# Forget gate kept as eight rows: a narrow projection, one scan over time, and its bias in the attention logits as a 128-row matmul

## The reference, cut to what matters

```python
def hybrid_mixer(h, w_in, b_f, ...):
    z = h @ w_in                                  # 256 x 4616
    zp, zq, zk, zv, zf, zx, zy = jnp.split(z, offsets, axis=-1)
    y_attn = forgetting_attention(zq, zk, zv, zf, b_f)   # zf: 256 x 8
# forgetting_attention, per head, with t the query and s the key:
#   F = cumsum(log_sigmoid(zf + b_f), axis=time)
#   logits[t, s] = (q[t] . k[s]) * scale + F[t] - F[s]     for s <= t
#   softmax over s, times v
```

## Time and profile before

| | |
|---|---|
| median of 3 runs | 3135.54 us (3131.29 to 3140.22) |
| the profiled execution | 3136.8 us, of which the span in the trace is 3135.0 us |
| PE busy | 3096.4 us, 99% of the span |
| DVE busy | 1981.1 us, 63% |
| ACT busy | 1481.2 us, 47% |
| mean granted TensorE clock | 0.990 |

### The profile page before, as it was taken

How to read it: one execution, slowest core, us unless ns; L and a number is a source line. 1 busy time by engine, 2 the same in 40 slices (tenths; PEclk the granted TensorE clock), 3 DMA queues, 4 the chain that set the end, 5 groups by cost and what they waited for, 6 DMA issues and landing times.

```text
span 3135.0 us, 38941 instructions
## 1 busy us (share of the span) xinstructions
PE 3096.4 (99%) x14466; PEld 2576.0 (82%) x14466; DVE 1981.1 (63%) x2086; ACT 1481.2 (47%) x1740; POOL 106.6 (3%) x206
## 2 busy tenths in 40 slices
PE   8999989999999999999999999999999999999999
PEld 7887868888888888888888888888888888888887
DVE  6778778975655655865564565556475555565564
ACT  5244535544444444545444444544545454444543
POOL 1211110100000000000000000000000000000000
PEclk9989999999999999999999999999999999999999
DMA  9978887965555555455556545555554555545555
GB/s 373 371 300 306 295 305 255 359 224 189 187 188 188 180 194 186 166 181 168 192 173 194 190 147 192 178 184 187 170 181 166 195 173 190 174 162 194 167 186 190
DMA packets 179990, 658.46 MB, mean 210 GB/s; under 512 B 20080, under 2 KB 20368, under 8 KB 179216
## 3 DMA queue, kind: packets, MB, share of 16 engines
q1 hardware_dynamic: 150992, 550.51, 52.1%
q0 software_dynamic: 28864, 106.08, 9.0%
HBM read 654.41 MB, written 2.10 MB: 209 GB/s over the span
## 4 chain that ended last, share of the span: by engine, by line
PE 96%; DMA 2%; DVE 1%; ACT 1%; issue 0%; SPq 0%; DVEq 0%; ACTq 0%
PE pg L1037 29%; PE pg L1039 29%; PE pg L1038 29%; PE pm L1072 2%; DMA w_raw<-w 1%; PE pm L1100 1%; PE pm L1558 1%; DMA R<-w_ada 1%; PE pm L1127 1%; PE pm L1452 0%; PE pm L1178 0%; PE pm L1177 0%; PE pm L1240 0%; PE pm L1135 0%; ACT w_hi L592 0%
## 5 line engine op out<-in xcount | busy, mean ns | idle before, releaser
L1607 DVE TENSOR_TENSOR w_lo<-w_raw,w_hi 128x1024 fp32r<-128x1024 f32 x888 | 1085.8, 1225 | 973.1 <-ACT w_hi L510 967.9
L510 ACT ACTIVATE w_hi<-w_raw 128x1024 fp32r<-128x1024 f32 x888 | 940.8, 1060 | 1328.5 <-PE pg L1039 1295.5
L1037 PE MATMUL pg<-w_hi,hT_hi 128*128 128x512 f32 x3232 | 1280.9, 396 | 18.5 <-DVE w_lo L1765 8.1
L1039 PE MATMUL pg<-w_hi,hT_lo 128*128 128x512 f32 x3232 | 1264.9, 391 | 0.0
L1038 PE MATMUL pg<-w_lo,hT_hi 128*128 128x512 f32 x3232 | 1264.3, 391 | 0.0
L1037 PEld LDWEIGHTS pg<-w_hi,hT_hi 128*128 128x128 f32 x3232 | 611.6, 189 | 146.4 <-issue 10.4
L1039 PEld LDWEIGHTS pg<-w_hi,hT_lo 128*128 128x128 f32 x3232 | 610.4, 189 | 129.6
L1038 PEld LDWEIGHTS pg<-w_lo,hT_hi 128*128 128x128 f32 x3232 | 611.5, 189 | 123.4 <-issue 0.5
L1037 PE MATMUL pg<-w_hi,y_parts 128*128 128x512 f32 x864 | 337.9, 391 | 1.4 <-issue 1.4
L1039 PE MATMUL pg<-w_hi,y_parts 128*128 128x512 f32 x864 | 336.4, 389 | 0.0
L1038 PE MATMUL pg<-w_lo,y_parts 128*128 128x512 f32 x864 | 336.1, 389 | 0.0
(11 more groups left out here) (281 smaller groups left out, 1380.3 us busy)
## 6 DMA issues: line engine op xcount, KB each, us to landing
w_raw<-w SPq DMA_DIRECT2D x1028, 512.0 KB, 3.7
R<-w_ada POOLq DMA_DIRECT2D x196, 512.0 KB, 7.4
R<-mem_T SPq DMA_DIRECT2D x4, 512.0 KB, 7.2
x_rows<-x SPq DMA_DIRECT2D x1, 2048.0 KB, 16.2
R<-mem_T SPq DMA_DIRECT2D x1, 2048.0 KB, 11.3
out<-x_rows SPq DMA_DIRECT2D x4, 512.0 KB, 5.8
con_sb<-con SPq DMA_DIRECT2D x1, 1344.0 KB, 16.0
small_w_sb<-small_w POOLq DMA_DIRECT2D x2, 576.0 KB, 5.8
```

Of the source, the lines that this page charges most:

```text
L510: act.activation(w_hi[:, g % RING, :, :].rearrange("p c n -> p (c n)"), raw[:, g % RING, :], ACT.Copy).then_inc(hi_done, 1)
L1037: pe.matmul(out, hi, w_hi[:, slot, c, :], start=start, stop=False)
L1039: return pe.matmul(out, lo, w_hi[:, slot, c, :], start=False, stop=stop)
L1607: tt(flat(w_lo[:, g % RING, :, :]), raw[:, g % RING, :], flat(w_hi[:, g % RING, :, :]).bitcast(F32), ALU.subtract).then_inc(lo_done, 1)
```

## The change

The gate is computed with the 8 gates on partitions and time along the row. The loaded side of the projection is now the 8 gate columns, split into `wf_hi` (ACT, at 35) and `wf_lo` (DVE, at 36), and the moving side is the activations that are already split (`hT_hi`, `hT_lo`), 256 columns at a time. Bias, minimum, `Exp`, `Ln` and the last subtraction work on 8x256, and one scan on DVE sums over time and writes `-F` straight into `F_row`. Two small transposes on PE make `F_t`. `F_row` is set to zero over all 128 partitions early on (DVE, at 11), and the bias matmul of the logits reads all 128 of its rows. `tri` is gone, so `con1` halves from 512 to 256 KB.

```diff
-        zf, logf, F_t = (sc[:, 240 + 16 * i:256 + 16 * i].rearrange("p (a h) -> p a h", a=TB) for i in range(3))
-        b_f = sc[:, 288:296]
+        zf, logf = view(12, S)[0:8, :], view(13, S)[0:8, :]
+        wf_hi, wf_lo = view_r(5, KD, 8), view_r(5.5, KD, 8)
+        F_t = sc[:, 240:256].rearrange("p (a h) -> p a h", a=TB)
+        b_f = sc[0:8, 288:289]
...
+            upto(35)
+            act.wait_ge(fw_in, 32)
+            act.activation(flat(wf_hi), flat(w_f), ACT.Copy).then_inc(wf_hi_done, 1)
...
-            act.activation(F_row[0:8, :], pm[2][0:8, 0:S], ACT.Copy, scale=-1.0).then_inc(F_sb, 1)
-            act.activation(flat(F_t), pm[2][:, S:S + TB * 8], ACT.Copy).then_inc(F_sb, 1)
+            act.activation(flat(F_t), pm[2][:, 0:TB * 8], ACT.Copy, scale=-1.0).then_inc(F_sb, 1)
...
-                        i = pe.matmul(out, ident[0:8, forget + h:forget + h + 1].to_broadcast([8, P]), F_row[0:8, :],
+                        i = pe.matmul(out, ident[:, forget + h:forget + h + 1].to_broadcast([P, P]), F_row,
                                       start=False, stop=True)
...
-            for tb in range(TB):
-                for k in range(KD):
-                    i = pe.matmul(pm[2][:, tb * 8:(tb + 1) * 8], hf_1[:, k, tb * P:(tb + 1) * P], w_f[:, k, :],
-                                  start=(k == 0), stop=(k == KD - 1))
+            pe.wait_ge(wf_ready, 1)
+            for k in range(KD):
+                out = pm[2][0:8, 0:S]
+                pe.matmul(out, wf_hi[:, k, :], hT_hi[:, k, :], start=(k == 0), stop=False)
+                pe.matmul(out, wf_lo[:, k, :], hT_hi[:, k, :], start=False, stop=False)
+                i = pe.matmul(out, wf_hi[:, k, :], hT_lo[:, k, :], start=False, stop=(k == KD - 1))
...
-            for sb_ in range(TB):
-                pe.matmul(pm[2][0:8, 0:S], logf[:, sb_, :], tri[:, sb_, :], start=(sb_ == 0), stop=(sb_ == 1))
             for tb in range(TB):
-                for sb_ in range(tb + 1):
-                    i = pe.matmul(pm[2][:, S + tb * 8:S + (tb + 1) * 8], tri[:, sb_, tb * P:(tb + 1) * P],
-                                  logf[:, sb_, :], start=(sb_ == 0), stop=(sb_ == tb))
+                i = pe.transpose(pm[2][:, tb * 8:(tb + 1) * 8], F_row[0:8, tb * P:(tb + 1) * P], ident[0:8, 0:8])
...
+            step(dve.memset(F_row, 0.0))
...
+            upto(36)
+            dve.wait_ge(wf_hi_done, 1)
+            tt(flat(wf_lo), flat(w_f), flat(wf_hi).bitcast(F32), ALU.subtract).then_inc(wf_ready, 1)
...
-            step(tt(zf, pm[2][:, 0:TB * 8].rearrange("p (a h) -> p a h", a=TB),
-                    b_f.unsqueeze(1).to_broadcast([P, TB, 8]), ALU.add))
-            step.settle()
-            step(ts(flat(F_t), flat(zf), -1.0, None, ALU.mult))
+            step(ts(zf, pm[2][0:8, 0:S], b_f, None, ALU.add))
             step.settle()
-            tt(flat(logf), flat(zf), flat(F_t), ALU.min).then_inc(zf_in, 1)
+            stt(logf, zf, -1.0, zf, ALU.mult, ALU.min).then_inc(zf_in, 1)
             upto(41)
             dve.wait_ge(zf_out, 2)
-            stt(flat(logf), flat(zf), 0.0, flat(logf), ALU.min, ALU.subtract).then_inc(logf_ready, 1)
+            step(stt(logf, zf, 0.0, logf, ALU.min, ALU.subtract))
+            step.settle()
+            dve.tensor_tensor_scan(F_row[0:8, :], ones[0:8, 0:1].to_broadcast([8, S]), logf, 0.0, ALU.mult, ALU.subtract
+                                   ).then_inc(F_ready, 1)
```

More of the change, by code:

```diff
@@ L155 @@
 _at = 0
-for _name, _n in (("causal", TB * S), ("tri", TB * S)):
+for _name, _n in (("causal", TB * S),):
     CON1[_name] = (_at, _at + _n)
@@ L311, in build @@
         causal = con1[:, 0:TB * S].rearrange("p (a s) -> p a s", a=TB)
-        tri = con1[:, TB * S:2 * TB * S].rearrange("p (a s) -> p a s", a=TB)
         pool_w = mv[:, 1, 0, :].rearrange("p (g d) -> p g d", g=4)
         F_row = mv[:, 1, 1, 0:S]
-        zf, logf, F_t = (sc[:, 240 + 16 * i:256 + 16 * i].rearrange("p (a h) -> p a h", a=TB) for i in range(3))
-        b_f = sc[:, 288:296]
+        zf, logf = view(12, S)[0:8, :], view(13, S)[0:8, :]
+        wf_hi, wf_lo = view_r(5, KD, 8), view_r(5.5, KD, 8)
+        F_t = sc[:, 240:256].rearrange("p (a h) -> p a h", a=TB)
+        b_f = sc[0:8, 288:289]
         w_f = small_w[:, 0:KD * 8].rearrange("p (k n) -> p k n", n=8)
@@ L389, in build @@
         lam_in, lam_out = map(sem, ("lam_in", "lam_out"))
-        zf_ps, zf_in, zf_out, logf_ready, F_ps, F_sb = map(
-            sem, ("zf_ps", "zf_in", "zf_out", "logf_ready", "F_ps", "F_sb"))
+        zf_ps, zf_in, zf_out, F_ready, F_ps, F_sb, wf_hi_done, wf_ready = map(
+            sem, ("zf_ps", "zf_in", "zf_out", "F_ready", "F_ps", "F_sb", "wf_hi_done", "wf_ready"))
         pool_ps, pool_sb = map(sem, ("pool_ps", "pool_sb"))
@@ L449, in _ @@
                 if g == 26:
-                    sp.dma_start(b_f, t["b_f"].partition_broadcast(P)).then_inc(fw_in, 16)
+                    sp.dma_start(b_f, t["b_f"]).then_inc(fw_in, 16)
                     sp.dma_start(small_w[:, 0:KD * 8 + 8 * P], t["front_w"]).then_inc(fw_in, 16)
@@ L688, in _ @@
             act.wait_ge(zf_in, 1)
-            act.activation(flat(logf), flat(logf), ACT.Exp).then_inc(zf_out, 1)
+            act.activation(logf, logf, ACT.Exp).then_inc(zf_out, 1)
             act.wait_ge(zf_out, 1)
-            act.activation(flat(logf), flat(logf), ACT.Ln, bias=1.0).then_inc(zf_out, 1)
+            act.activation(logf, logf, ACT.Ln, bias=1.0).then_inc(zf_out, 1)
             upto(43)
@@ L1246, in _ @@
             upto(42)
-            pe.wait_ge(cons1_in, 16 * 2)
-            pe.wait_ge(logf_ready, 1)
-            for sb_ in range(TB):
-                pe.matmul(pm[2][0:8, 0:S], logf[:, sb_, :], tri[:, sb_, :], start=(sb_ == 0), stop=(sb_ == 1))
+            pe.wait_ge(F_ready, 1)
             for tb in range(TB):
-                for sb_ in range(tb + 1):
-                    i = pe.matmul(pm[2][:, S + tb * 8:S + (tb + 1) * 8], tri[:, sb_, tb * P:(tb + 1) * P],
-                                  logf[:, sb_, :], start=(sb_ == 0), stop=(sb_ == tb))
+                i = pe.transpose(pm[2][:, tb * 8:(tb + 1) * 8], F_row[0:8, tb * P:(tb + 1) * P], ident[0:8, 0:8])
             i.then_inc(F_ps, 1)
             upto(46)
-            pe.wait_ge(F_sb, 2)
+            pe.wait_ge(F_sb, 1)
             pe.wait_ge(evac_act, F_ACTS[FRONT.index("y")])
@@ L1921, in _ @@
             take_mod(5, 3)
-            dve.wait_ge(F_sb, 2)
+            dve.wait_ge(F_sb, 1)
+            dve.wait_ge(cons1_in, 16 * 2)
             attn_at(73, 0, S1, causal, 0)
@@ L2417, in constants @@
     con1[:, 0:TB * S] = np.where(s[None, None, :] <= t[:, :, None], 0.0, FAR).reshape(P, -1)
-    con1[:, TB * S:2 * TB * S] = (t[:, :, None] <= s[None, None, :]).reshape(P, -1)
     band = np.zeros((P, TB, 4, S), np.float32)
@@ L2504 @@
         "w_ada": np.stack(ada),
-        "b_f": a["b_f"][0], "final_g": a["final_g"],
+        "b_f": a["b_f"][0][:, None], "final_g": a["final_g"],
         "pool_w": a["pool_w"][0].transpose(1, 0, 2),
```

## The result

The changed kernel takes 3120.27 us (median of 5 runs, 3117.05 to 3122.06) against 3135.54 (5 runs, 3131.29 to 3140.22): ratio 0.9948, 95% interval 0.9933 to 0.9963. Its profiled execution took 3122.06 us, with a span of 3120.2 us: 14.8 less than the 3135.0 of before.

What follows compares the result with a forecast made beforehand. PE, busy for 99% of the span, was taken as the bound. 4.56 + 0.35 + 9.5 + 3.2 + 0.3 = 17.9 us off 3136.8 gives 3118.9, less 1.3 to the median, said as 3118; 3110 to 3126 holds 0.8.

Steps and rivals of the forecast that it cites:

- Projection: Gate projection on PE: 48 passes with 8 loaded columns take 5.83 us instead of 10.39, gaining 4.56 us.
- The rival of narrow passes that don't overlap: Gate projection: with 8 loaded columns each pass pays 0.2 us, 9.6 us more, 3127.5 us; chance 0.05.
- From the gate to tile 44: Projection's end to tile 44: shorter PE work would gain 2.7 us, but waiting for DVE leaves 0.35 us.
- the new wait: At tile 44: PE waits about 2.4 us for DVE's w_lo, as DVE has more to do ahead of it.
- elsewhere PE idled for 2.54 us in such a place and the clock stayed at 1.00: Wait at tile 44: one row elsewhere taken as sign that it costs 2.4 us alone, without a clock fall.
- First logits and the tile behind: First logit stretch 13.71 to 6.7 us, gaining 7.0, and 2.5 from the tile behind: 9.5 us together.
- second logits: Second logit stretch: 16 matmuls, all with 128 rows, take 6.7 us instead of 9.91, gaining 3.2 us.
- Rows don't matter: Logits: widening from 8 to 128 rows leaves matmul time unchanged, only the gate gives 5.2 us, about 3130; chance 0.07.
- The clock falls all the same: First logits: the clock still falls 5.6 us in, taking 3.6 us from the gain, 3121.5 us; chance 0.10.
- A wide broadcast load is slow: Logits: 128-row loads repeating one column outlast their matmul; at 1 us each 3150 us, slower than before; chance 0.03.
- The rest: con1 loses 256 KB where the DMA engines are full: 0.3 us taken, 0.6 at most; other small changes nothing.

Runs made afterwards that it cites:

- run 3: Changed kernel without a w_ada sum on DVE at tiles 40 and 42, two each at 52 and 54, sums between moved by one or two tiles: 3116.06 us.
- run 1: Kernel before with only the logits changed: F_row zeroed and the bias matmul over 128 rows, gate as it was: 3125.61 us, ratio 0.9964.
- run 2: Changed kernel with the logits' bias matmul back on 8 rows and no zeroing, so only the gate is changed: 3133.02 us, ratio 0.9991.
- Run 4: Changed kernel with 8-row bias matmuls in the logits, grouped as four heads' products, then four heads' biases, per token block: 3119.44 us, ratio 0.9948.
- run 5: Changed kernel with the logits' bias matmul over 64 rows instead of 128: 3125.66 us, ratio 0.996.
- run 6: As run 3, with the zeroing of the feed-forward accumulator moved from ahead of that part's first w_lo to 16 tiles later: 3113.02 us, ratio 0.9919.
- run 7: Changed kernel with the gate as 16 f32 matmuls in place of 48 split passes, the split of its weights left out: 3121.45 us, ratio 0.9949.
- run 8: The changed kernel again, unaltered, for a second trace: one execution, 3121.73 us, span 3119.9.
- the first group: The first four follow-up runs, measured together with the kernel before beside them: 3136.43 us, 23 runs.

## Why the prediction came out as it did

The forecast was 3118.0 us, in a range of 3110 to 3126; measured is 3120.27, inside it. The sum was 17.9 us, the traces give 14.8; most of the difference is two falls of the clock, 1.74 and 1.67 us, that the sum didn't have. Step by step:

- **Projection**, 4.56 forecast, 4.92 measured. The pace of the 72-column passes holds for 8 columns (5.47 / 48 = 0.114 us); the 0.2 for changes of shape was not due, since the loaded rows stay 128. The rival of narrow passes that don't overlap is out.
- **From the gate to tile 44**, 0.35 forecast, 0.46 measured, and the new wait 2.4 forecast, 2.37 measured. That is the step with the most terms, and its parts were right: DVE's two longer operations took 0.88 us where I took 0.86, the third 0.41 for 0.47, the scan 0.68 for 0.67, all at 8 partitions where the forecast took rows at 128. That the wait came out so well is also because what PE would have had to itself, 17.98, was right to 0.1 us (20.24 - 2.37 = 17.87).
- **"elsewhere PE idled for 2.54 us in such a place and the clock stayed at 1.00" is the step that failed.** It was one row, and that row was an exception: in 13 of the 15 waits of the table above the clock fell. Behind tile 44 that costs 1.74 us by the timeline; run 3, without the wait, doesn't have it. The forecast had the fall in neither its sum nor its rivals. The trace of before itself had waits of PE that spoke against it. In PE's timeline:

```profile
122.91 1.90 PE L1127 MATMUL pm<-sc,R 128*128 128x1 f32 x11 [1.79 <-DMA R<-w_ada]
...
158.89 1.87 PE L1135 MATMUL pm<-con_sb,R 128*128 128x1 f32 x8 [1.98 <-DVE R L1679]
```

The clock is at 0.50 over 124 to 125 and over 159 to 161 us. What PE resumes with here moves one column per matmul, fewer still than the 8 of the gate, so these rows can't say whether it is the wait or the narrow matmuls; but they were a reason not to count on 1.00.
- **The same row also hid a second term.** The kernel before had been let off at the feed-forward wait; the changed one wasn't, in either trace, which is the -1.67 at the end of the span. It needs neither half of the change: run 1 leaves the gate as it was, run 2 the logits, and both lost the clock there. Whether the kernel before mostly loses it too, one trace can't say.
- **First logits and the tile behind**, 9.5 forecast, 9.44 measured, and **second logits**, 3.2 and 3.19. Run 4 and run 5 show the cause that the prediction gave. *Rows don't matter* was right about rows alone and wrong about the time, since what costs is the change between shapes. *The clock falls all the same* didn't happen in the logits: of the 14 stretches in seven traces without a change of shape at every matmul (after, runs 1, 3, 4, 6, 7, 8) none has a fall, of the six that alternate (before, runs 2 and 5) three do, all three with 8 rows: three of four, against none of two with 64. It happened at tile 44 instead. *A wide broadcast load is slow*: it loads at the pace of its neighbour.
- **The rest**, 0.3 for `con1`, was never measured by itself. The 0.72 us at the projection's start can't be put to it: that start lies between 181.6 and 185.2 us over the traces, and the time lost to the clock from 100 us up to it between 8.5 and 12.0.
- **The 0.52 us between the second logits and the feed-forward wait** is low clock behind the long wait near 450 us, which the forecast took to move along unchanged. PE's timelines after and before:

```profile
451.69 0.79 PE L1040 MATMUL pg<-w_hi,hT_hi 128*128 128x512 f32 x1 [7.70 <-DVE x_rows L1756]
...
468.73 0.80 PE L1037 MATMUL pg<-w_hi,hT_hi 128*128 128x512 f32 x1 [7.84 <-DVE x_rows L1756]
```

Over the 10 us from there the granted clock is 0.78 on the mean after and 0.85 before, 2.2 and 1.5 us lost; 0.6 more, less the 0.14 by which the wait is shorter, is about the 0.52. In the second trace of the changed kernel (run 8) it is 0.74, so this too varies from execution to execution.

The profiled execution before had its large fall in the first logits, which the kernel need not have every time, and 6.3 us of the forecast rested on that one execution. On the average it is less: the 23 executions of before in the first group lost 30.5 us to the clock and the ten of run 1 25.9, so the logits give 4.6 us of clock back. That the forecast landed within 2.3 us of the median doesn't mean that every step was right: two falls, 3.4 us, were missing from the sum, and the range was wide enough to hold them.

## What to carry to other kernels

Look at the shape that is loaded in neighbouring small f32 matmuls: each change between 8 or 64 and 128 rows costs 0.21 us here, so either pad the short one with zeros to 128 rows or group matmuls of one shape, whichever the order of consumers allows. Zeros to 128 and grouping were the same in time here (3120.27 and 3119.44 us). When a step is made shorter on PE, ask what the helper engine still owes at the next tile, and price a PE wait of some 2.4 us amid dense matmuls at 4.1, not 2.4 (run 3 gained 4.2 in the medians by taking one away). A single row in which the clock was spared is one draw: count such places over several traces before a sum rests on it.

## What was not expected of the hardware

- A wait of 2.2 to 2.5 us brought a stretch of half clock that cost 1.4 to 1.7 us in 13 of 15 cases, beginning within 0.8 us of the moment that PE resumed, before or after it; waits of 0.26 and 0.48 us at the same tile (runs 3 and 6) never did, nor did waits of 1.0 us for another `w_lo` and of 1.4 us near 1250 us that all ten traces have.
- Matmuls with 8 moving columns lost the clock in two traces of two, while PE's records show no idle time; with 256 moving columns, f32 or not, in none of eight. With 8 and 128 loaded rows in turn it was three stretches of four, with 64 and 128 in turn none of two, at the same pace.
- 64 loaded rows beside 128 cost exactly what 8 do: 0.62 us per f32 matmul of 256 columns against 0.43.
